# Six heads a column group, 512-column key products, gate pages on SP's queue, a bf16 mask, and two tokens a partition in the cached pages

## The reference

```python
# sample group, layer 0: an indexer picks 256 of 2049 positions, attention over those
sel = top_k(indexer_scores(qi, wi, ki_all), 256)
s = einsum('qkgd,qnkd->qkgn', q, k_sel) * 128**-0.5 - slopes * dist      # 12 heads, 2 KV heads
# sample group, layer 1: attention over all 2048 cached tokens and the new one
k_all = concat(pool_k[page_table], k_new); v_all = ...; lf_all = ...     # 12 heads, 4 KV heads
cg = cumsum(lf_all)                                                      # log forget gates, 12 a token
s = einsum('bqkgd,blkd->bkgql', q, k_all) * 128**-0.5 + c_q - c_k
# both: softmax, o = p @ v; 4 more heads attend to 256 memory tokens
h = layer_norm(ALPHA * h + concat(heads) @ w_o)
h = layer_norm(ALPHA * h + moe(h))                                       # 16 experts, top 2 of one group
```

## Time and profile before

| | |
|---|---|
| median of 3 runs | 2226.7 us (2223.63 to 2236.98) |
| profiled execution, its time | 2235.39 us |
| its span | 2233.6 us |
| granted clock of TensorE, mean | 0.973 |
| PE busy | 2110.6 us, 94% of the span |
| DVE, ACT busy | 768.9 and 387.1 us |
| DMA | 647.49 MB, mean 290 GB/s |

### The profile page before, as it was taken

The page is one execution under the profiler, slowest core; times in us unless marked ns, Lnnn a source line. Parts: engine busy times, 40 slices in busy tenths (PEclk is TensorE's granted clock), DMA queues, the critical chain, the costliest instruction groups (busy, mean ns, idle before and its releaser), DMA issues.

```text
span 2233.6 us, 34908 instructions
## 1 busy us (share of the span) xinstructions
PE 2110.6 (94%) x13909; PEld 1315.5 (59%) x13909; DVE 768.9 (34%) x1262; ACT 387.1 (17%) x932; POOL 8.2 (0%) x11
## 2 busy tenths in 40 slices
PE   9999998999999999999887988899999999999999
PEld 7778785688733444343566867645787444453534
DVE  0239996401751222222400433423016522222223
ACT  1221103400421001111301100133104211100112
POOL 0000000000000000000000000000000000000000
PEclk9999999999999999999998999989999999999999
DMA  9744586873189999999762576898742699999994
GB/s 274 232 147 124 196 261 215 258 280 145 69 352 426 419 427 416 427 414 426 267 195 77 176 257 245 293 383 295 250 151 76 279 425 420 427 425 429 414 426 178
DMA packets 213862, 647.49 MB, mean 290 GB/s; under 512 B 55400, under 2 KB 88953, under 8 KB 184161
## 3 DMA queue, kind: packets, MB, share of 16 engines
q1 hardware_dynamic: 180673, 637.39, 74.0%
q10 hardware_dynamic: 33056, 8.27, 1.9%
HBM read 639.62 MB, written 5.96 MB: 289 GB/s over the span
## 4 chain that ended last, share of the span: by engine, by line
PE 74%; DMA 11%; SPq 6%; DVE 3%; issue 3%; ACTq 1%; ACT 1%; DVEq 0%
PE bank L714 15%; PE bank L1395 13%; PE bank L1194 10%; PE bank L1442 8%; DMA ring<-in_w_down 6%; PE bank L1456 6%; SPq L413 4%; DMA ring<-in_w_up 4%; PE bank L1368 4%; PE bank L944 3%; PE bank L1071 2%; DVE ring L2132 1%; ACTq L413 1%; DMA ring<-in_cache_b_k 1%; PE bank L1278 1%
## 5 line engine op out<-in xcount | busy, mean ns | idle before, releaser
L1395 PE MATMUL bank<-ring,AT 128*64 128x512 f32 x2048 | 457.1, 596 | 11.8 <-DMA ring<-in_w_up 8.6
L714 PE MATMUL bank<-X,ring 128*128 128x264 f32 x1664 | 390.4, 392 | 6.2 <-ACT X L1818 6.2
L714 PEld LDWEIGHTS bank<-X,ring 128*128 128x128 f32 x1664 | 315.3, 193 | 66.2 <-issue 13.7
L1395 PEld LDWEIGHTS bank<-ring,AT 128*64 128x64 f32 x2048 | 145.7, 137 | 283.9 <-issue 269.4
L1567 ACT ACTIVATE arena<-bank 128x512 f32<-128x512 f32 (+11 forms) x311 | 137.1, 479 | 793.6 <-PE bank L714 252.0
L1442 PE MATMUL bank<-ring,arena 128*64 128x512 f32 x1024 | 224.7, 594 | 21.9 <-ACT arena L1567 13.8
L2523 DVE TENSOR_TENSOR X<-bank,X 128x264 f32<-128x264 f32 x256 | 110.8, 433 | 365.6 <-PE bank L1456 363.7
L1194 PE MATMUL bank<-AT,ring 128*128 128x264 f32 x1024 | 232.7, 390 | 0.0
L1194 PEld LDWEIGHTS bank<-AT,ring 128*128 128x128 f32 x1024 | 196.8, 193 | 34.1
L2132 DVE STREAM_TRANSPOSE ring<-ring 128x4096 f32<-128x4096 f32 x24 | 106.5, 4442 | 194.6 <-DMA ring<-in_cache_b_k 190.1
L1442 PEld LDWEIGHTS bank<-ring,arena 128*64 128x64 f32 x1024 | 74.7, 137 | 161.5 <-issue 152.0
(11 more groups left out here) (347 smaller groups left out, 1352.6 us busy)
## 6 DMA issues: line engine op xcount, KB each, us to landing
ring<-in_w_gate SPq DMA_DIRECT2D x64, 2048.0 KB, 15.9
ring<-in_w_up SPq DMA_DIRECT2D x48, 2048.0 KB, 15.6
ring<-in_w_down SPq DMA_DIRECT2D x48, 2048.0 KB, 13.2
ring<-in_w_o SPq DMA_DIRECT2D x16, 2048.0 KB, 11.7
ring<-in_w_up SPq DMA_DIRECT2D x32, 1024.0 KB, 7.6
ring<-in_w_down SPq DMA_DIRECT2D x32, 1024.0 KB, 15.8
ring<-in_cache_b_k SPq DMA_DIRECT2D x128, 256.0 KB, 5.1
ring<-in_cache_b_v SPq DMA_DIRECT2D x128, 256.0 KB, 4.9
```

The costliest lines, as they stand in the source:

```text
L714: mm = pe.matmul(B[at + f][:, 0:n_tok], u[:, c * 512 + f * P:c * 512 + (f + 1) * P], src[8 * half + c][:, 0:n_tok], start=(half == 0 and c ...
L1395: mm = pe.matmul(B[bank][64 * s:64 * s + 64, :], M.xsT[:, at:at + 64], ring[slots[s][0]][:, c * FE:(c + 1) * FE], start=(half == 0 and c = ...
```

## The change

1. **Rows of scores.** A sequence has two column tiles in place of one, six heads (`HALF`) in each, and four sequences share a tile.
2. **Key products.** A group is two sequences. In both layers each product covers 16 pages, 512 columns. Layer 0 has four groups of 64 products (before, two of 128), layer 1 four groups of 128 (before, four of 256). In layer 0 they stand after the slab `qm`, after each `mkv` slab, and at the end. `late_rows` moves into the middle of the last group. In layer 1 the two ring places of a sequence must be neighbours, so `plan` names places, and the second of each pair is given up by a tiny transpose after the group.
3. **Gates.** ACT no longer issues them. SP does, into the plain tile `a.LC`, after three units of the plan (`GATES_AFTER`), and DVE moves them to their rows (`place_gates`, four copies).
4. **Mask** in bf16 with a bf16 `to12`.
5. **Pages.** `load_pages(..., tokens=2)` puts two tokens on a partition: a page of keys or values goes to 64 partitions, pages with even number to partitions 0 to 63 and those with odd number to 64 to 127, in rows of 2 KB (layer 0) or 4 KB (layer 1), where before it went to all 128 in rows of 1 KB or 2 KB.
6. **What follows from these.** Values: two products of half the columns for each page. Turning the probabilities: 32 products of 64 rows with every second column in place of 16 transposes. ACT waits for its stores before the third memory-key copy, not before the copies to `PT`, since `MN` (the memory keys to be stored) lies elsewhere.

```diff
+GATES_AFTER = {("kv", 2): (0, 1, 2), ("mem", 0): (3, 4), ("q", 5): (5, 6, 7)}
-def score_row(b):
-    return 32 * (b % 4) + 8 + H * (b // 4)
+def score_row(b, h):
+    return 32 * (2 * (b % 2) + h // HALF) + 8 + HALF * (b // 2) + h % HALF
...
-        u += units("q", range(4, 6)) + units("kv", range(2)) + units("k", range(4), 8)
-        u += units("qm", range(2)) + units("k", range(4, 8), 8)
-        u += units("mkv", range(2)) + units("k", range(8, 12), 8)
-        u += units("mkv", range(2, 4)) + units("k", range(12, 16), 8) + units("mk", range(2), 4)
-        u += units("v", range(16), 8) + units("mv", range(2), 4)
+        u += units("q", range(4, 6), 1, 0) + units("kv", [0], 1, 5) + units("kv", [1], 1, 2)
+        for x, name in enumerate(("qm", "mkv", "mkv", "mk")):
+            k, n = (2 if x == 2 else 0), (4 if name == "mk" else 1)
+            u += units("k", range(4 * x, 4 * x + 2), 8, 3) + units("k", range(4 * x + 2, 4 * x + 4), 8, 0)
+            u += units(name, [k], n, 5) + units(name, [k + 1], n, 2)
+        u += units("v", range(16), 8, 3) + units("mv", range(2), 4)
...
-            a.MN = work[:, 1024:2048]
+            a.mask = work[0:NB, 2048:3072].bitcast(BF16)
+            a.MN = AT[:, 3072:4096]
...
-                    eng.dma_start(dst(g + k), cache[bass.ds(page, 1)].rearrange("a p w -> (a p) w")).then_inc(sem, 16)
+                    eng.dma_start(dst(g + k), cache[bass.ds(page, 1)].rearrange("a (p j) w -> (a p) (j w)", j=tokens))\
+                       .then_inc(sem, 16)
...
+            def page_place(t, W, g):
+
+                return t[64 * (g % 2):64 * (g % 2) + 64, g // 2 * 2 * W:(g // 2 + 1) * 2 * W]
...
+                    if layer == 1 and (name, k) in GATES_AFTER:
+                        if GATES_AFTER[name, k][0] == 0:
+                            sp.wait_ge(S("ln_out"), 2 * KC)
+                        for b in GATES_AFTER[name, k]:
+                            pages(S("lf_in"), b, 0, PAGES, i["cache_b_lf"][0],
+                                  lambda g: lay[1].LC[:, (g * NB + b) * H:(g * NB + b + 1) * H])
...
+                steps = [(j, d) for j in range(a.nk // 2) for d in range(4)]
+                for x, (j, d) in enumerate(steps):
+                    if between and x == len(steps) // 2:
+                        between()
+                    for b in seqs:
+                        for f in range(2):
+                            kv = f * (a.nk // 2) + j
+                            q = ((2 * d + kv % 2) * NB + b) * 32
+                            out = slice(32 * (2 * (b % 2) + f), 32 * (2 * (b % 2) + f) + 32)
                             for r in range(4):
                                 rows = slice(32 * r, 32 * r + 32)
-                                mm = pe.matmul(B[bank + r][out, 32 * first:32 * (first + per)],
-                                               a.Qz[kv // 2][rows, at:at + 32],
-                                               tile[rows, :, kv * P + 32 * d:kv * P + 32 * d + 32],
+                                mm = pe.matmul(B[bank + r][out, :], a.Qz[kv // 2][rows, q:q + 32],
+                                               tiles[b][rows, :, kv * P + 32 * d:kv * P + 32 * d + 32],
...
+                if layer == 1:
+                    pe.wait_ge(S("slab_copied"), cnt["slab"])
+                    pe.wait_ge(S("natural_copied"), cnt["natural"])
+                    for b in seqs:
+                        leave(pe.transpose(B[other + 3][0:32, 480:512], ident[0:32, 0:32], ident[0:32, 0:32]),
+                              layer, "k", n * b + 1)
...
-                        mm = pe.transpose(B[bank + j][:, pg * P:(pg + 1) * P], a.S[:, (4 * j + pg) * P:(4 * j + pg + 1) * P], ident)
+                        for h in range(2):
+                            at = 2 * P * (2 * j + pg // 2) + P * h + pg % 2
+                            mm = pe.matmul(B[bank + j][64 * h:64 * h + 64, pg * P:(pg + 1) * P], a.S[:, at:at + P - 1:2], ident,
+                                           start=True, stop=True)
...
+                    def product(pg, p, v):
+                        for f in range(2):
+                            c, g = 32 * (2 * (b % 2) + f), (17 * b + pg + 2 * f) % 4
+                            mm = pe.matmul(out[32 * g:32 * g + 32, f * w:(f + 1) * w], p[:, c:c + 32], v[:, f * w:(f + 1) * w],
+                                           start=(pg < 2), stop=(pg >= PAGES - 1))
...
                     slab(layer, "mkv", 0, Ac, SEQ, 4)
+                    key_products(layer, a, 1)
                     slab(layer, "mkv", 1, Ac, SEQ, 4)
-                    key_products(layer, a, 1)
+                    key_products(layer, a, 2)
+                    key_products(layer, a, 3, lambda: late_rows(layer, a))
...
+                    if m == 2:
+                        act.wait_ge(S("stored"), 16 * stores[0])
...
-                act.wait_ge(S("stored"), 16 * stores[0])
...
                     queries(0, 0)
                     gate_rows(a)
-                    load_lf(range(2, 4))
                     queries(1, 4)
-                    load_lf(range(4, 6))
                     turn_rows(Ac, 4)
```

More of the change, by code:

```diff
@@ L112, in const_table @@
     add("to12", own12.T)
-    add("fold12", np.concatenate([i[:, None] % 32 == 8 + H * q + np.arange(H)[None] for q in range(2)], 1))
+    add("fold6", np.concatenate([i[:, None] % 32 == 8 + HALF * q + np.arange(HALF)[None] for q in range(NB // 2)], 1))
     j = np.arange(2 * HM)
@@ L207, in sb @@
             return ctx.enter_context(nc.sbuf_tensor(name, [rows, cols], dt))
-        ring = [sb(f"ring{k}", UNIT) for k in range(RING)]
+        places = sb("ring", RING * UNIT)
+        ring = [places[:, k * UNIT:(k + 1) * UNIT] for k in range(RING)]
         X = sb("X", KC * T)
@@ L540, in _ @@
                         b, first, per = key_unit(layer, k)
-                        pages(full(layer, s), b, first, per, ck, lambda g: t[:, (g - first) * W:(g - first + 1) * W])
+                        pages(full(layer, s), b, first, per, ck, lambda g: page_place(t, W, g - first), 2)
                     elif name == "v":
@@ L923, in gate_rows, with key_products @@
                       .then_inc(S("lf_rows"), 1)
-            def key_products(layer, a, group):
-                per = UNIT // a.W
-                bank = key_banks(layer)
-                us = range(4 * group, 4 * group + 4)
+            def key_products(layer, a, group, between=None):
+                n = (1, 2)[layer]
+                bank, other = key_banks(layer), other_banks(layer)
+                seqs = (2 * group, 2 * group + 1)
                 if group == 0:
@@ L933, in key_products @@
                         pe.wait_ge(S("lf_copied"), 4)
-                pe.wait_ge(S("keys_made"), key_base(layer) + us[-1] + 1)
-                tiles = [ring[units[layer]["k", u][0]][:, :].rearrange("p (g w) -> p g w", w=a.W) for u in us]
-                for kv in range(a.nk):
-                    for d in range(4):
-                        for u, tile in zip(us, tiles):
-                            b, first, _ = key_unit(layer, u)
-                            at = ((2 * d + kv % 2) * NB + b) * 32
-                            out = slice(32 * (b % 4), 32 * (b % 4) + 32)
+                pe.wait_ge(S("keys_made"), key_base(layer) + n * (seqs[1] + 1))
@@ new lines, in key_products @@
+                at = {b: units[layer]["k", n * b][0] * UNIT for b in seqs}
+                tiles = {b: places[:, at[b]:at[b] + n * UNIT].rearrange("p (g w) -> p g w", w=a.W) for b in seqs}
+                steps = [(j, d) for j in range(a.nk // 2) for d in range(4)]
[7 more added lines that the diff above has]
+                            out = slice(32 * (2 * (b % 2) + f), 32 * (2 * (b % 2) + f) + 32)
@@ L949, in key_products @@
-                            if kv == a.nk - 1 and d == 3:
-                                leave(mm, layer, "k", u)
+                                mm = pe.matmul(B[bank + r][out, :], a.Qz[kv // 2][rows, q:q + 32],
+                                               tiles[b][rows, :, kv * P + 32 * d:kv * P + 32 * d + 32],
+                                               start=(b < 2 and x == 0),
+                                               stop=(layer == 1 and b >= NB - 2 and x == len(steps) - 1))
@@ L952, in sample_scores @@
+                        if x == len(steps) - 1:
+                            leave(mm, layer, "k", n * b)
+                if layer == 1:
[4 more added lines that the diff above has]
+                              layer, "k", n * b + 1)
             def sample_scores(layer, a):
@@ L1076, in values @@
                     if half:
-                        g = (17 * b + PAGES) % 4
-                        pe.matmul(out[32 * g:32 * g + 32, 0:a.W], a.PTn[:, 32 * (b % 4):32 * (b % 4) + 32], a.VNs,
-                                  start=False, stop=True).then_inc(S("ov_ready"), 1)
+                        product(PAGES, a.PTn, a.VNs).then_inc(S("ov_ready"), 1)
```

104 lines of the change are left out of this document (56 added, 48 removed).

## The result

| | before | after |
|---|---|---|
| median of 12 runs each | 2235.24 us | 2253.15 us (2242.4 to 2257.19) |
| ratio, 95% interval | | 1.0085 (1.0063 to 1.0107) |
| span of the profiled execution | 2233.6 us | 2248.2 us |
| granted clock of TensorE, mean | 0.973 | 0.964 |

One of the 12 runs of the kernel before took 3118.67 us and is left out of the ratio.

What follows compares the result with a forecast made beforehand. PE, busy 94% of the span, was taken as the bound, by its work and gaps. Terms -27.4 - 17.6 - 2.4 - 3.0 - 6.7 + 2.0 = -55.1 us gave 2172 us against the median 2226.7; range 2150 to 2230.

Steps and rivals of the forecast that it cites:

- the one on the rate: Layer 1's key transfers: 4 KB rows move 386 to 421 GB/s, at 403 a group's transfer takes 20.8 us, not 21.7.
- rival 1: Key and value pages on half the partitions could load at half the rate, up to 2303 us; chance 0.17 below 250 GB/s.
- the break-even of 245: Page rate in GB/s near which longer waits (three of 12.5 us) and values (17 us) eat the 55 us gain.
- Layer 0, -6.7: Layer 0's attention: SP starts the values 6.7 us sooner and stays the limit, so the last arrive 6.7 us sooner.
- Gates, -27.4: Start of layer 1: both PE gaps behind ACT's copies go, 23.66 us, and some 3.7 us of slow products behind them.
- the cover: SP's 128 added gate pages cost nothing, hidden under some 17 us before PE asks for `mem`.
- Key products, -17.6: Layer 1's four key groups take 11.0 us each, 44.1 in place of 62.66; two tiny transposes a group add about 1.
- Late rows, -2.4: After layer 1's fourth key group: moved inside the last group, ACT's copies lie beside products; between 0 and -4 us.
- Waits behind slabs, -3: Layer 1's three PE waits for key units: about 1 us less each through faster transfers; 0 to -9.4 us.
- Added to PE, +2: Values in more products, turning probabilities and ACT's earlier wait for stores: +2 us for all, 0 to 10.
- Rivals 2 and 3: 2: layer 1 key groups keep 15.7 us, 2190 us, chance 0.08; 3: gates' pages delay `mem`, 2182 us, chance 0.05.

Runs made afterwards that it cites:

- experiment 1: Probe of DMAs alone, no kernel, by destination partitions: 8.39 MB took 24.3 us on 128 partitions, 38.3 on halves in turn, 24.6 on every second.
- experiment 7: Changed kernel with one token a partition, the 128 gate pages issued by ACT again: 2189.44 us.
- experiment 8: Changed kernel with one token a partition, each layer 1 key product split in two of 256 columns: 2191.45 us.
- experiment 3: Changed kernel with two-token pages on every second partition instead of halves: 2190.42 us, 0.9805 of the kernel before.
- experiment 2: Changed kernel with one token a partition again, key and value pages on all 128 partitions: 2161.04 us, 0.969 of the kernel before.

## Why the prediction was wrong

**The step that failed** is the one on the rate: "With 4 KB rows the rate should lie between 386 and the 421 of the long rows; at 403 it is 20.8 us", and with it the weight of 0.52 for the forecast and 0.17 for rival 1. The price of a transfer to half of the partitions was said to be unknown, and then I filled it in from rows with full pages, by the length of a row. Measured: 235 GB/s, below the break-even of 245. Rival 1's arithmetic held for the waits and the values: 14 us on each wait at 231 GB/s, the estimate by the Trainium skill's figure of 6% (SBUF — State Buffer, "Can I just issue two DMAs to hit both halves?") (measured +13.9, +11.7 and +13.5), 30 on the values (the stretch grew by 26.9). That its end, 15 to 20 us above before, was met too (+17.9 by the medians) is partly luck: layer 0 came out 12 us worse than in that sum, and the key products, the waits and the values some 11 us better. The argument against the rival, that 32 queued pages in short pieces would overlap, was worth 8 to 10% (experiment 1).

**Layer 0, -6.7: wrong too, and by a mechanism that I did not have.** Measured +5.5. The earlier start was there, 11.3 us instead of 6.7, but 64-partition pages take SP longer to issue, 0.77 us in place of 0.63. "Layer 0 needs only 207 and is not touched at that rate" looked at the engines alone, in a stretch that I had just called issue-bound. With one token, layer 0's attention ends 9.2 us sooner than before. The mask went from 7.03 to 1.25 us, a little more than forecast.

**Gates, -27.4: right.** From layer 1's first product to its first key product 185.13 us became 156.69, -28.4; experiment 7 puts 28 us on it. SP issued `mem` at 1137.86, and PE asked for it at 1165.19 without a wait; the cover held.

**Key products, -17.6: right in kind, too small.** 40.0 us against 62.66 is -22.6. The 11.0 us a group came from layer 0's two groups with their pauses (9.63 busy of 10.66); now 128 records in a row take 4.47 us, 256 take 8.69, and of "issue" pauses 0.8 us are left in all groups. So 13 of the 22.6 us are pauses, which the forecast named as a direction, and 10 are PE's own time (49.63 us busy before). That half the records must have half the pauses doesn't hold: experiment 8 has the old number of records and 1.5 us of pauses. Nor is a pause the price of each block of 128 records and their weight loads, as the forecast read it: in layer 1 the changed kernel runs groups of 256 records with none.

**Late rows, -2.4: right.** They take 3.2 us inside the last group; 5.83 stood behind it before.

**Waits behind slabs, -3: wrong, +39.** See the rate. With one token they are 8.66 us, 0.7 better than before; the -3 rested on a higher rate by longer rows. The engines have it (387 GB/s with 2 KB rows, 410 to 417 with 4 KB, over 128 partitions, experiment 1), but no kernel here could use it: two-token pages in the halves don't reach it, and on every second partition SP asks for 355 GB/s at most (experiment 3).

**Added to PE, +2: right for the work, but the clock was left out.** Turning the probabilities takes 3.72 us a layer in place of some 2, and the 128-column products of layer 0 take 17.5 us in experiment 2, near the forecast 18. ACT's wait before the third memory-key copy costs nothing: PE's longest wait there is 2.98 us in both kernels. What I had no term for is the slow clock. "36.0 against 35.9: nothing" became 45.7 us beside the waits for values, 9.8 us more; with 17.9 us more of idle time these are the 26.9 us by which layer 1's attention grew, less 0.8 in its other work. In the one-token kernel it works the other way: the clock there is 0.94 against 0.89 before, the same products take 33.1 us, and the stretch is 10.3 us shorter. Another 3.3 us of that are a gain that the forecast overlooked: the products for the new token, split in two column tiles, take 5.0 us in place of 8.3.

**Rivals 2 and 3** fell: groups are near 10 us, and there is no gap at `mem`. The sum without the fifth item is -52 us (the -3 goes). The one-token kernel is 70 us faster than the kernel before by the medians of one session, 2161.04 against 2231.47: the terms beside the pages were right in kind and 18 us too small. The forecast's 2172 looks closer than that only because it stands on 2226.7, the median of three runs; 12 runs gave 2235.24, so the 8.7 us taken off for the profiled execution had no ground.

## What to carry to other kernels

In these probes the destination's partitions set the rate of a DMA before its row length did (40% against 7%): look at which halves a transfer writes, not at how many partitions. When no row of the trace prices something that a change newly depends on, and a stated rule does, the rule deserves more weight than an interpolation between rows that don't have the property at all; a probe of a dozen lines settles it. A queue that is bound by issue needs the issue time of the new shape checked as well as its rate. And one item of a bundle can eat the others' gain: split it before judging it.

## What the runs showed of the hardware

- 8.39 MB in pages to alternating halves ran at 234 GB/s, to one half at 217, to 32 neighbouring partitions at 221; to every second or every fourth partition, 376 and 380, as fast as 128 partitions at 377. Two queues, one for each half, reached 294 (315 late in the phase).
- Late in a phase, 128 partitions moved 387 GB/s with 2 KB rows and 410 to 417 with 4 KB rows.
- Issuing a DMA with 64 destination partitions took SP 0.63 to 0.65 us in the probes, with 16, 32, 96 or 128 neighbouring ones 0.44 to 0.50; 512 KB over 128 partitions took 0.58, and every fourth partition 0.63. In the kernels a page took 0.74 to 0.79 us on 64 partitions.
- Splitting 32-row products of 512 columns into two of 256, one behind the other on the same tile, cost 31 us for 1024 more records, 30 ns each. In another order such records took 21 ns.
- The same 512 records took 45.7 us at a granted clock of 0.84 over the stretch and 33.1 at 0.94.
